# A rebuilt state-space stage: new order of units, decay rows by DMA, half a unit in each pair of heads

## The reference, cut to what matters

```python
def ssd_mixer(xn, in_w, conv_w, conv_b, dt_bias, a_log, d_skip, norm_g, out_w):
    proj = xn @ in_w                       # z 2048, x 2048, B and C 4*128 each, dt 32
    xbc = silu(causal_dwconv(xbc, conv_w, conv_b))
    dt = softplus(dt + dt_bias);  dA = dt * -exp(a_log)
    a_cs = cumsum(dA);  lmat = exp(a_cs_l - a_cs_s) below the diagonal
    y_diag = (C B^T * lmat) (x * dt);  states = B^T (decay * x * dt)
    y_off = C h_in * exp(a_cs);  y = y_diag + y_off + x * d_skip
    yg = rmsnorm per group of 512 (y * silu(z)) * norm_g
    return yg @ out_w
```

## Time and profile before

| | us |
|---|---|
| median of three runs | 1878.51 (1876.03 to 1881.35) |
| the profiled execution | 1881.36 |
| its span | 1879.6 |
| TensorE busy | 1823.6 (97%) |
| VectorE busy | 1323.8 (70%) |
| ScalarE busy | 985.5 (52%) |

### The profile page before, as it was taken

One profiled execution on the slowest core, in us unless ns is written; L12 is line 12 of the kernel. 1 busy time (PEld: TensorE's weight loads), 2 busy tenths in 40 slices (PEclk: granted clock), 3 DMA queues, 4 the chain that ended last, 5 costly groups with the idle time before them and its releaser, 6 DMA issues.

```text
span 1879.6 us, 33229 instructions
## 1 busy us (share of the span) xinstructions
PE 1823.6 (97%) x13529; PEld 1729.2 (92%) x13529; DVE 1323.8 (70%) x1676; ACT 985.5 (52%) x1168; POOL 5.4 (0%) x34
## 2 busy tenths in 40 slices
PE   6989899999999999999999999999999999999998
PEld 6988799999889999999999999998989999999997
DVE  5968677778788777786667566666756666776665
ACT  5744455456656554565446445444545445565443
POOL 1000000000000000000000000000000000000000
PEclk9999999999999999999999999999999999999999
DMA  6542155555533555555555454555645564445552
GB/s 190 181 133 91 46 179 180 179 189 197 162 117 107 177 180 179 191 175 186 187 186 172 158 179 157 196 175 188 188 131 197 180 200 145 148 138 199 191 175 82
DMA packets 237961, 310.50 MB, mean 165 GB/s; under 512 B 8226, under 2 KB 213800, under 8 KB 237864
## 3 DMA queue, kind: packets, MB, share of 16 engines
q1 hardware_dynamic: 236520, 308.03, 49.5%
q10 hardware_dynamic: 1344, 1.09, 0.2%
HBM read 308.04 MB, written 1.06 MB: 164 GB/s over the span
## 4 chain that ended last, share of the span: by engine, by line
PE 92%; DVE 4%; ACT 2%; issue 1%; DMA 0%; SPq 0%; DVEq 0%; ACTq 0%
PE ps L630 17%; PE ps L609 11%; PE ps L611 11%; PE ps L610 11%; PE ps L658 9%; PE ps L660 9%; PE ps L661 9%; PE ps L632 9%; DVE weights_lo L1838 1%; ACT weights_hi L1211 1%; PE ps L909 1%; PE ps L810 1%; PE ps L761 0%; PE ps L895 0%; PE ps L824 0%
## 5 line engine op out<-in xcount | busy, mean ns | idle before, releaser
L1838 DVE TENSOR_TENSOR weights_lo<-raw_weights,weights_hi 128x2048 fp32r<-128x2048 f32 x275 | 629.3, 2289 | 252.7 <-ACT weights_hi L1211 251.6
L1211 ACT ACTIVATE weights_hi<-raw_weights 128x2048 fp32r<-128x2048 f32 x283 | 538.8, 1905 | 235.3 <-DVE scratch L1891 96.8
L609 PE MATMUL ps<-normed,weights_hi 128*128 128x256 f32 x1792 | 522.5, 292 | 11.4 <-DVE normed L1931 7.2
L610 PE MATMUL ps<-normed,weights_hi 128*128 128x256 f32 x1792 | 509.7, 284 | 0.0
L611 PE MATMUL ps<-normed,weights_lo 128*128 128x256 f32 x1792 | 509.6, 284 | 0.0
L630 PE MATMUL ps<-normed,weights_hi 128*128 128x512 f32 x1408 | 500.5, 399 | 2.7 <-DVE normed L1931 2.4
L658 PE MATMUL ps<-down_in_hi,weights_hi 128*128 128x256 f32 x1440 | 411.5, 286 | 3.6 <-DVE down_in_lo L1952 3.4
L660 PE MATMUL ps<-down_in_lo,weights_hi 128*128 128x256 f32 x1440 | 408.5, 284 | 0.0
L661 PE MATMUL ps<-down_in_hi,weights_lo 128*128 128x256 f32 x1440 | 408.4, 284 | 0.0
L632 PE MATMUL ps<-normed,weights_lo 128*128 128x256 f32 x1408 | 395.8, 281 | 0.0
L609 PEld LDWEIGHTS ps<-normed,weights_hi 128*128 128x128 f32 x1792 | 346.4, 193 | 16.7 <-issue 10.9
(11 more groups left out here) (251 smaller groups left out, 1356.5 us busy)
## 6 DMA issues: line engine op xcount, KB each, us to landing
raw_weights<-in_ffn_w_gate_up_dram SPq DMA_DIRECT2D x88, 1024.0 KB, 5.1
raw_weights<-in_ffn_up_w_dram SPq DMA_DIRECT2D x44, 1024.0 KB, 5.1
raw_weights<-in_ffn_w_down_dram SPq DMA_DIRECT2D x44, 1024.0 KB, 4.9
raw_weights<-in_ffn_down_w_dram SPq DMA_DIRECT2D x22, 1024.0 KB, 4.9
raw_weights<-in_ssd_in_w_dram SPq DMA_DIRECT2D x20, 1024.0 KB, 5.3
raw_weights<-in_a_w_in_dram SPq DMA_DIRECT2D x14, 1024.0 KB, 5.1
raw_weights<-in_attn_in_w_dram SPq DMA_DIRECT2D x12, 1024.0 KB, 5.4
raw_weights<-in_ssd_out_w_dram SPq DMA_DIRECT2D x8, 1024.0 KB, 4.9
```

Source lines behind the costliest of these rows:

```text
L609: mm(o, hi, h_hi[:, k, :], start=(k == 0 and a == 0), stop=False, skip_group_check=True)
L610: mm(o, hi, h_lo[:, k, :], start=False, stop=False, skip_group_check=True)
L1211: f(w_hi[:, s, :], raw[:, s, :], ACT.Copy).then_inc(hi_split.sem, hi_split.plus())
L1838: tt(w_lo[:, s, :], raw[:, s, :], f32(w_hi[:, s, :]), ALU.subtract).then_inc(lo_split.sem, lo_split.plus())
```

## The change

- **Order.** B and C are the first four units, then x of the first group (two), then z and x alternate: `SSD_ORDER` has sixteen entries, twelve xbc and four z (at indices 6, 9, 12, 15). STREAM follows it, and ScalarE and VectorE run it unrolled. `conv_in` and `conv_out` become one buffer each, in `proj`. VectorE gives its missing split at index 6.
- **Decays.** The small product stands behind unit 3, its transposes behind unit 5, `softplus` at index 6, the sums behind unit 8. B is transposed and multiplied with C behind unit 6. x of group 0 is transposed before and behind unit 11 and read by VectorE at indices 11 and 12; `new_state` stands before units 14 and 15.
- **Decay rows.** One product gives the cumulative sums of all heads as rows; VectorE copies them out, ScalarE's queue stores them to DRAM and loads them back, broadcast to all partitions, two rows per pair, four pairs ahead. `head_rows` is gone. `segments` is two 128x256 minima, and the exponential becomes four of 128x128 with a bias column.
- **Pairs.** Every pair has half a unit: four z units in pairs 0 to 7, four down units in pairs 8 to 15. Group norms are done inside pairs 5 to 15. Two PSUM banks take turns for `heads_out`. Four down units remain behind the pairs, with the last square sum behind the first of them.

The core of the diff:

```diff
-Z_WOVEN = 4
+SSD_ORDER = [("xbc", j) for j in (8, 9, 10, 11, 0, 1)] + [("z", 0), ("xbc", 2), ("xbc", 3), ("z", 1), ("xbc", 4), ("xbc", 5),
+             ("z", 2), ("xbc", 6), ("xbc", 7), ("z", 3)]
+ROW_RING = 4
...
@@ TensorE, ssd_core and the main order
-                def head_rows(p):
-                    for q in range(2):
-                        for a in range(TH):
-                            col = 32 * a + 2 * p + q
-                            last = mm(ps[:, 1 + p % 3, (2 * q + a) * P:(2 * q + a + 1) * P],
-                                      dA[:, col:col + 1].to_broadcast([P, P]), upper[:], start=True, stop=True)
...
+            def decay_sums():
+                pe.wait_ge(dA_ready.sem, dA_ready.next())
+                mm(ps[:, STAT, 0:64], upper[:], dA, start=True, stop=True)
+                mm(ps[:, STAT, 64:96], ones[:], dA[:, 0:32], start=True, stop=True)
+                for a in range(TH):
+                    last = mm(ps[0:SSD_HEADS, STAT, T + a * P:T + (a + 1) * P], dA[:, 32 * a:32 * a + 32], upper[:],
+                              start=True, stop=True)
...
+                def half_unit(p):
+                    j, half = p // 2, range(4 * (p % 2), 4 * (p % 2) + 4)
+                    if j < 4:
+                        up_unit(ks=half, b=j, reused=False)
+                        return
...
+                    down_unit(first=(j == 4), ms=half, begin=(p % 2 == 0), end=(p % 2 == 1))
...
+            more_ups(2)
+            pe.wait_ge(setup_read.sem, setup_read.next(2))
             small_product(SSD_HEADS)
+            more_ups(2)
+            turn_small(SSD_HEADS, total=ssd_small_sum)
             up_unit()
+            turn_b()
+            more_ups(2)
+            decay_sums()
+            more_ups(2)
+            pe.wait_ge(in_ready.sem, in_ready.next(2))
+            turn_x(0, 0, 3)
             up_unit()
+            pe.wait_ge(bank_free.sem, bank_free.next())
+            turn_x(0, 1, 0)
+            more_ups(2)
+            pe.wait_ge(cb_read.sem, cb_read.next())
+            pe.wait_ge(bank_free.sem, bank_free.next())
+            new_state(0, 1)
+            more_ups(2)
+            ssd_pairs()
...
 @@ ScalarE
+            for i, (kind, j) in enumerate(SSD_ORDER):
+                if kind == "xbc":
+                    one_unit(conv_xbc, j, late=silu_xbc)
+                else:
+                    one_unit(j=j, late=silu_z)
...
+                elif i == 11:
+                    act.wait_ge(rows_stored.sem, rows_stored.value())
+                    for p in range(ROW_RING):
+                        load_rows(p)
...
-                f(seg[p % 3], seg[p % 3], ACT.Exp).then_inc(decay_ready.sem, decay_ready.plus())
+                for q in range(2):
+                    for a in range(TH):
+                        col, m = 32 * a + 2 * p + q, seg[p % 3][:, q, a * P:(a + 1) * P]
+                        last = f(m, m, ACT.Exp, bias=neg_acs[:, col:col + 1])
+                if p and p + ROW_RING - 1 < SSD_PAIRS:
+                    act.wait_ge(row_exp.sem, row_exp.value())
+                    load_rows(p + ROW_RING - 1)
...
+                if p in (5, 10):
+                    for j in range(2):
+                        act.wait_ge(evacuated.sem, evacuated.next())
+                        activate_z(4 + j + 2 * (p // 10))
+                    logs_and_exps()
...
@@ VectorE
+            for i, (kind, j) in enumerate(SSD_ORDER):
+                s = i % RING
+                if kind == "z":
+                    dve.wait_ge(su_done.sem, su_done.next())
+                    to_proj(0)(j, s)
+                    if i == 6:
+                        split_next()
+                    split_next()
+                else:
+                    conv_xbc(j, s, split_next if i else lambda: None)
+                if i == 3:
+                    norm_small(SSD_HEADS, ssd_small_sum)
+                elif i == 6:
+                    head_decays()
+                elif i == 7:
+                    take_b()
+                elif i == 9:
+                    decay_columns()
...
+                elif i == 11:
+                    x_first(0, 3)
+                elif i == 12:
+                    x_second(0, 0)
...
                 for q in range(2):
-                    for a in range(TH):
-                        col, at = 32 * a + 2 * p + q, (2 * q + a) * P
-                        ins = ts(seg[p % 3][:, q, a * P:(a + 1) * P], ps[:, 1 + p % 3, at:at + P],
-                                 a_cs[:, col:col + 1], 0.0, ALU.subtract, ALU.min)
+                    ins = tt(seg[p % 3][:, q, :].rearrange("p (a t) -> p a t", a=TH),
+                             decay_rows[p % ROW_RING][:, q, :].rearrange("p (a t) -> p a t", a=TH),
+                             each(pair_acs[:, p, q, :], P), ALU.min)
```

More of the change, by code:

```diff
@@ L838, in ssd_core @@
[L838 to L846, removed]
                 for p in range(SSD_PAIRS):
-                    if p + 2 < SSD_PAIRS:
-                        head_rows(p + 2)
+                    if p == 1:
+                        pe.wait_ge(evacuated.sem, evacuated.value(-1))
@@ L867, in softmax_attention @@
+                    if p >= 5 and p % 4 == 1:
+                        square_sum(p // 4 - 1)
+                down_unit()
+                square_sum(3)
+                down_unit()
+                down_unit()
+                down_unit(last=True)
             def softmax_attention(kinds, between=lambda n: None, ending=lambda: None):
@@ L1168, in _ @@
             row_exp = c("row_exp")
+            rows_copied = c("rows_copied")
+            rows_stored = c("rows_stored", step=16)
+            rows_landed = [c(f"rows_landed{i}", step=16) for i in range(ROW_RING)]
             rstd_ready = c("rstd_ready")
@@ new lines, in _ @@
+                g = (p - 5) // 4
+                if p >= 5 and p % 4 == 1:
+                    group_square(g)
+                elif p >= 6 and p % 4 == 2:
+                    group_root()
+                elif p >= 7 and p % 4 == 3:
+                    feed_out(2 * g)
+                elif p >= 8 and p % 4 == 0:
+                    feed_out(2 * g + 1)
+            group_square(3)
+            feed_out(5)
+            for _ in range(2):
+                act.wait_ge(su_done.sem, su_done.next())
+                split_next()
@@ L1566, in _ @@
+            group_root()
+            feed_out(6)
+            feed_out(7)
+            for _ in range(2):
+                act.wait_ge(su_done.sem, su_done.next())
+                split_next()
             norm("norm_ffn_g", 0, ahead=True, wide=False)
@@ L1790, in _ @@
             row_exp = c("row_exp")
-            rows_done = c("rows_done")
+            rows_copied = c("rows_copied")
+            rows_landed = [c(f"rows_landed{i}", step=16) for i in range(ROW_RING)]
             rstd_ready = c("rstd_ready")
@@ L2208, in _ @@
             small_weights(SSD_HEADS)
-            conv_xbc(0, slot[0], lambda: None)
-            with c.repeat(3, per_trip(evacuated=3, conv_base=3, conv_done=3, vec_step=15)) as i:
-                for j in range(RING):
-                    conv_xbc(i * RING + (1 + j), (slot[0] + 1) % RING, lambda: split_next(3))
-            for j in (10, 11):
-                conv_xbc(j, (slot[0] + 1) % RING, split_next)
-            split_next()
-            norm_small(SSD_HEADS)
-            one_unit(to_proj(0), 0)
@@ L2250, in x_first, with take_b @@
+            def take_b():
+                dve.wait_ge(turned.sem, turned.next())
+                v.tensor_copy(flat(b_tok), ps[:, 0, :]).then_inc(bank_free.sem, bank_free.plus())
+                dve.wait_ge(cb_done.sem, cb_done.next())
+                for a in range(TH):
+                    ins = tt(cb[:, :, a, :], bank(1 + a, 4), rows(upper[:], 4), ALU.mult)
+                ins.then_inc(cb_read.sem, cb_read.plus())
+            def x_first(g, b):
                 hs = slice(8 * g, 8 * g + 8)
```

290 lines of the change are left out of this document (152 added, 138 removed), and 3 rows, old and new, of the table STREAM.

## The result

The changed kernel takes **1887.46 us** (median of five runs, 1883.12 to 1892.48) against 1878.51 (also of five runs): the ratio is 1.0049, with a 95% interval from 1.0028 to 1.007: slower by about 0.5%, and the interval does not reach 1.

What follows compares the result with a forecast made beforehand. TensorE held 92% of the chain before; VectorE and ScalarE would then set the pace in two places. Stage end 150.7 + 97.8 + 25.1 = 273.6 against 264.1, +9.5 on median 1878.51: 1888.0 us, range 1869 to 1897.

Steps and rivals of the forecast that it cites:

- Front, units 0 to 6: Start of the stage: a table load goes, first convolution 1.3 us earlier; unit 6 ends at 65.9, VectorE's index 6 at 75.65.
- Front, units 7 to 15: Each convolution unit becomes one serial ScalarE-VectorE chain of 8.48 us, before 5.7; first heads_out at 150.7 against 137.3, +13.4 us.
- The pairs: Sixteen head pairs: 92.8 us from work of TensorE, VectorE and ScalarE, plus 5.0 for falls of the clock: 97.8.
- The rest: Behind the pairs: a down unit 5.77 us, the last square sum 2.0, three down units 17.3: 25.1, no wait expected.
- The table load's drain: ScalarE's table switches: the skill's extra 1.38 us each would make the sum about 5 us higher; the forecast left it out.
- Rival 1: Front: high half in time, convolution units near 5.7 us, heads_out near 126, stage end near 242: 1856 us; chance 0.12.
- Rival 2: Front as forecast, but pairs near TensorE's pace, 80 us, with VectorE's steps hidden: -8, 1870 us; chance 0.15.
- rival 3: Effects cancel: exponentials and handovers a little cheaper, no falls of the clock: -3 to +3, 1878 us; chance 0.08.
- rival 4: Dearer: clock at 1.2 GHz through much of the pairs, or row loads land late: +20, 1898 us; chance 0.10.

Runs made afterwards that it cites:

- the four kernels named above: The changed kernel with, one each: transposes of x ahead of heads_out (1880.25 us), row loads by GpSimd (1882.28), one exponential for four (1885.93), gates copied without SiLU (1884.83).
- the best version: The changed kernel with transposes of x ahead of heads_out and the missing low split moved from index 6 to VectorE's pair 1: 1859.09 us, ratio 0.9911.
- the first experiment: The changed kernel with the missing low split given at index 15 in place of index 6, so VectorE stays one unit behind ScalarE: 1867.3 us, ratio 0.9933.

## Why the prediction was right

It said 1888.0, and the median is 1887.46. That is closer than its steps were, and so partly luck. The signs that it named were there: VectorE idle 3.01 us for the copy in every convolution unit from index 7 on, the two long waits of TensorE, pairs of 6.2 to 7.0 us where x is taken (7.95 in pair 10), and no wait in front of the cumulative sums. In the profiled executions the stage ends 6.6 us later, where +9.5 was forecast. The medians differ by 8.95 us, but the profiled execution of before was itself 2.9 us above its median and that of after is not. Among the profiled executions the forecast was 1890.9, and 1887.4 was measured: 3.5 us too high, 2.9 of it in the stage. Step by step:

- **Front, units 0 to 6: 1.6 us too short for the profiled execution.** The table load in front of the first Identity did go and the wait before 41 shrank to 0.9 us. But the wait at 26.5 was 1.51 us instead of 1.2, and the clock fell behind it, which the earlier trace rows had not shown for 1.2 us. VectorE's evacuation at index 7 came at 77.23 instead of 75.65. In the four kernels named above, without that fall, it came at 75.59 to 75.92: the step was right for the kernel, and wrong in taking a clock that stays up as certain. The stretch behind that wait:

```profile
26.50:30.30 3.80, 3.79 (x19) 3.79 (x20) 2.16 (x1) 0.21 (x1) 0.00 (x0) 0.56 0.67 201
```

- **Front, units 7 to 15: right, the step that decides.** The chain of 8.48 us was found at 8.28 and 8.48 (indices 8 and 10). Index 11 took 9.47, not 10.7: the 1.0 us for the SiLU table load was mis-sized. The load at 104.70 stands directly behind the copy and ahead of the wait for the taps, so it lies in ScalarE's idle 3.42 us. The four row loads did take 1.80 us of issue, but began at 117.91, beside VectorE's reads of x, so only part came on the path: 1.4 us by the kernel with GpSimd's issue. x_second ended at 124.6 (forecast 125.65). From the evacuation at index 7 to there it took 47.4 us instead of 50.0, and these −2.6 us more than cancel the +1.6 before them. TensorE's stops were 11.7 us (about 13 forecast) and 10.5 (about 11), and the first `heads_out` came at 150.01 against 150.7.
- **The pairs: right in the mechanism, 1.9 us too long.** They took 95.9 us against 97.8 (the last pair, which ends in no start of another, is counted at the forecast's 4.05 in this sum and in those of the other kernels). By fours, forecast without clock falls and measured: 21.2 and 22.0; 25.6 and 25.9; 26.2 and 28.7; 19.75 and 19.35. The misses are pair 9 (6.05 forecast, 7.25 measured, with the clock down) and pair 11 (5.65 and 6.66). The falls of the clock were booked at +5.0 and the sum is 3.1 above that without any, all causes together. Of the four pairs for which a fall was booked (5, 7, 9 and 11), it came in 9 and 11 only; and one fall costs 1.4 to 1.8 us where 1.5 or 1.0 was booked (last section). Pair 0 took 6.54 us against 6.0. The single issue of a row load was booked at 0.45 us and took 0.33.
- **The rest** took 24.8 us against 25.1, and the square sum behind the first down unit brought no wait. From 249 on TensorE is busy all the time.
- **The table load's drain** that the Trainium skill (ScalarE: Activation LUTs, What ACT_TABLE_LOAD costs) adds to a switch is again not seen: in pair 10 the activations start 0.02 and 0.01 us after the end of their loads, 213.59 and 216.05. Without both loads the root comes 2.83 us sooner after the copy (5.69 less 2.86), and the two loads themselves are 2.56 of that.
- **The rivals.** Rival 1, that the handover does not bind, was false for the change. Its condition came true when the lag was kept: the first `heads_out` at 131.1 (126 worked out), the stage's end at 254.4 (242) and 1867 us (1856). Only with the turn of x first and the split in pair 1 as well does the time come near its price: 1859 us. Rival 2 (80 us of pairs) was not met; with x turned first they take 89.8. Nor were rival 3 (no falls of the clock, 1878) and rival 4 (1898): the clock was 0.95 over the pairs, and the row loads landed 3.0 to 5.5 us after their issue, and no engine waited for them in the pairs.

In the pairs of the best version TensorE is busy 83.5 of 92.5 us. The 9 us left are waits for VectorE's masks, but for 1.1 before pair 12 ("issue"). TensorE's waits there, 16 to 280 us:

```profile
PE ps L836 <- DVE scratch L2365: 10.8, 7, 3.3
```

Of these 10.8 us 3.0 stand before the first `heads_out`. The longest, 3.3, stands behind pair 10, the pair with the table loads; the others are 0.6 to 1.2. What would remove them stays open.

## What to carry to other kernels

When two engines split one stream of work, count for each iteration whether the second needs what the first makes in the same iteration, and whether the first waits for the second ahead of making it. If both are so, the times add up (8.28 and 8.48 us a unit at indices 8 and 10, instead of 5.65 and 6.25 with the lag kept), and neither engine's busy share shows it. A lag of one iteration between them is worth keeping; catch up only where the second engine has nothing to do. And what TensorE hands over with few instructions (four transposes) belongs ahead of the long product of the same step, if the other engine's work on it is the longer chain (here 1.3 to 1.7 us in each of four pairs). And before a difference between two profiled executions is put down to an edit, look whether it is there already ahead of the edited place, as 1.5 us were here.

## What the runs showed of the hardware

- **Equal waits, unequal clocks.** In the execution of after two waits of TensorE are alike:

```profile
178.86 0.43 PE L838 MATMUL ps<-mem_v,scratch 128*64 128x128 f32 x2 [2.25 <-DVE scratch L2367]
...
204.74 0.69 PE L838 MATMUL ps<-mem_v,scratch 128*64 128x128 f32 x2 [2.24 <-DVE scratch L2367]
```

  Behind the first the granted clock was 1.00, behind the second 0.79, and the first matmuls show it too (0.43 against 0.69 us). The stretches:

```profile
178.80:184.80 6.00, 5.94 (x45) 5.28 (x46) 3.90 (x9) 4.59 (x8) 0.00 (x0) 1.00 0.61 206
...
204.70:212.00 7.30, 7.26 (x45) 6.43 (x45) 4.40 (x9) 1.92 (x2) 0.00 (x0) 0.79 0.58 179
```

  In the first experiment the wait of 2.24 us before pair 5 was followed by 0.77, and the one of 2.43 before pair 7 by 0.60, where after had 2.43 and 1.00. Pair 7 behind its wait of 2.43 us, in after and then with the row loads by GpSimd:

```profile
191.70:197.90 6.20, 5.06 (x38) 4.21 (x38) 5.02 (x12) 3.63 (x8) 0.00 (x0) 1.00 0.50 182
```

```profile
189.20:195.40 6.20, 6.19 (x26) 4.83 (x27) 3.19 (x7) 2.11 (x6) 0.00 (x0) 0.50 0.50 170
```

  The pair took 6.13 us in the first and 7.97 in the second. In the same way pair 5 took 5.87 or 7.39 us and pair 9 5.87 or 7.25: one fall costs 1.4 to 1.8 us here. Even behind the longest of these waits, 3.35 us before pair 11, the clock was 0.75 in after and 1.00 with the row loads by GpSimd. So a wait of this length makes a fall possible, not certain, and a sum should carry it as a range. The Trainium skill (TensorE: Matmul & The Clock Gate, HAM oscillation) describes a kernel that waits for a transfer in every trip of a loop and whose clock falls anew each time. The waits here recur too, and the runs agree for some of them and not for others; over all pairs of after the granted clock was 0.95.
- **A short wait can do it too**: at the same place near 26.5 us the clock was 0.56 behind 1.51 us in after and 0.55 behind 1.57 with the copy first; it was 1.00 behind 1.2 us before and behind 0.3 to 1.1 in the other kernels.
- **The issue of a row load on ScalarE's queue** takes 0.33 us alone and 0.45 each when four stand in a row (1.80 for four).
